# The delta rule's triangular inverse: blocks up to 32 in a compact 32-column form

## What is computed

```python
a_mat = jnp.einsum('bnhid,bnhjd->bnhij', k_beta, k) * decay * strict
sol = lax.linalg.triangular_solve(eye + a_mat, rhs, left_side=True, lower=True, unit_diagonal=True)
u, w = sol[..., :dv], sol[..., dv:]
```

## Time and profile before

| | us |
|---|---|
| median of 3 runs | 1971.06 (1970.66 to 1971.6) |
| span of the profiled execution | 1968.8 |
| one turn of the mixer loop with a chain (7 of them) | 68.6 |
| VectorE busy in such a turn | 57.3 |
| ScalarE busy in such a turn | 36.4 |
| GpSimd busy in such a turn | 1.1 |
| granted TensorE clock, mean | 0.997 |
| a load of 1024 KB of weights, from issue to landing | 5.1 |

### The profile page before, as it was taken

One profiled execution on the slowest core, in us unless ns is written; L12 is line 12 of the kernel. 1 busy time (PEld: TensorE's weight loads), 2 busy tenths in 40 slices (PEclk: granted clock), 3 DMA queues, 4 the chain that ended last, 5 costly groups with the idle time before them and its releaser, 6 DMA issues.

```text
span 1968.8 us, 30310 instructions
## 1 busy us (share of the span) xinstructions
PE 1940.8 (99%) x10837; PEld 1691.3 (86%) x10837; DVE 1289.1 (65%) x2362; ACT 984.7 (50%) x1930; POOL 28.4 (1%) x52
## 2 busy tenths in 40 slices
PE   8999999999999999999999999999999999999996
PEld 7889999999999988888888788888888888888885
DVE  6558788888878856565566697555555555555554
ACT  4446455545545535454444464544544444544442
POOL 1000000000000000000000000000000000000000
PEclk9999999999999999999999999999999999999998
DMA  8666455345445446566556555665555555665551
GB/s 314 198 159 182 124 127 147 107 118 149 111 128 133 161 142 243 193 198 199 191 191 240 172 192 188 197 201 185 187 191 191 192 192 182 223 204 195 194 195 68
DMA packets 203603, 349.51 MB, mean 178 GB/s; under 512 B 6704, under 2 KB 72448, under 8 KB 202512
## 3 DMA queue, kind: packets, MB, share of 16 engines
q1 hardware_dynamic: 200272, 334.13, 51.6%
q0 software_dynamic: 3264, 14.47, 4.5%
HBM read 344.19 MB, written 2.10 MB: 176 GB/s over the span
## 4 chain that ended last, share of the span: by engine, by line
PE 95%; DVE 2%; ACT 1%; issue 1%; DMA 0%; DVEq 0%; SPq 0%
PE dense L549 23%; PE dense L551 23%; PE dense L550 23%; PE dense L537 6%; PE dense L539 6%; PE dense L538 6%; PE chain L675 1%; PE chain L696 1%; PE chain L766 1%; PE chain L951 0%; ACT sE L1145 0%; PE chain L776 0%; PE chain L784 0%; DMA raw<-in_w_in_dram 0%; PE chain L639 0%
## 5 line engine op out<-in xcount | busy, mean ns | idle before, releaser
L1306 DVE TENSOR_TENSOR lo<-raw,hi 128x512 fp32r<-128x512 f32 x1256 | 849.9, 690 | 502.3 <-ACT hi L994 500.0
L994 ACT ACTIVATE hi<-raw 128x512 fp32r<-128x512 f32 x1256 | 780.7, 631 | 694.0 <-PE dense L551 622.9
L549 PE MATMUL dense<-hi,xh 128*128 128x512 f32 x1376 | 539.8, 392 | 1.9 <-DVE xl L1839 1.1
L551 PE MATMUL dense<-lo,xh 128*128 128x512 f32 x1376 | 535.9, 389 | 0.0
L550 PE MATMUL dense<-hi,xl 128*128 128x512 f32 x1376 | 535.5, 389 | 0.0
L549 PEld LDWEIGHTS dense<-hi,xh 128*128 128x128 f32 x1376 | 258.4, 188 | 55.2 <-DVE xl L1839 2.0
L551 PEld LDWEIGHTS dense<-lo,xh 128*128 128x128 f32 x1376 | 258.2, 188 | 54.2
L537 PE MATMUL dense<-xh,hi 128*128 128x256 f32 x1024 | 304.4, 297 | 0.0
L550 PEld LDWEIGHTS dense<-hi,xl 128*128 128x128 f32 x1376 | 258.5, 188 | 52.5
L539 PE MATMUL dense<-xh,lo 128*128 128x256 f32 x1024 | 289.6, 283 | 0.0
L538 PE MATMUL dense<-xl,hi 128*128 128x256 f32 x1024 | 289.3, 283 | 0.0
(11 more groups left out here) (290 smaller groups left out, 1521.5 us busy)
## 6 DMA issues: line engine op xcount, KB each, us to landing
raw<-in_w_in_dram SPq DMA_DIRECT2D x116, 1024.0 KB, 5.1
raw<-in_w_ffn_gate_dram SPq DMA_DIRECT2D x44, 1024.0 KB, 5.1
raw<-in_w_ffn_up_dram SPq DMA_DIRECT2D x44, 1024.0 KB, 5.1
raw<-in_w_ffn_down_dram SPq DMA_DIRECT2D x44, 1024.0 KB, 5.0
raw<-in_w_br_att_dram SPq DMA_DIRECT2D x16, 1024.0 KB, 5.0
raw<-in_w_br_dn_dram SPq DMA_DIRECT2D x16, 1024.0 KB, 5.0
raw<-in_w_out_dram SPq DMA_DIRECT2D x16, 1024.0 KB, 5.0
raw<-in_w_ple_gate_dram SPq DMA_DIRECT2D x16, 1024.0 KB, 5.0
```

What stands on the lines that cost most here:

```text
L549: pe.matmul(o, ah, hi[:, s, :], start=(k == 0), stop=False)
L551: mm = pe.matmul(o, ah, lo[:, s, :], start=False, stop=(k == nk - 1))
L994: act.activation(hi[:, pos.slot(n), :], raw[:, slot, off:off + 512], ACT.Copy).then_inc(sem("hi_ready"), 1)
L1306: dve.tensor_tensor(lo[:, pos.slot(n), :], raw[:, slot, off:off + 512], hi[:, pos.slot(n), :].bitcast(F32), ALU.subtract).then_inc(sem("lo ...
```

## The change

Levels 0 to 4 no longer work on 128 columns. In a compact form only the diagonal 32x32 blocks are kept: `VU` holds, for each of the four matrices, three blocks of 32 columns (what is left of A's own diagonal block as a level's input, the neighbour block for the level from 32 to 64, and the inverse so far). One level is then one product of 96 columns for each of the four matrices, with a stationary matrix `Ym` (a negated level part plus, in the constant mask, the identity):

- ScalarE, step 3 (`packed`): six copies of 32 partitions x 128 columns out of `AT` into `VU`.
- GpSimd (`inverse_seed`), for each pair: a copy and two elementwise instructions on 128 columns, behind `packed`. The next `G` is loaded behind them.
- VectorE, step 5 (`FIRST`): `level_matrix`, a transpose of 128 columns and a masked product of 512 columns, for level 0. The three instructions of level 0 in step 2 are gone.
- TensorE: `inv_level` in steps 6, 8, 10, 12, 14 (96 columns) and 16 (32 columns, level 5). Steps 9, 11, 13, 15 and 17 have no chain product any more, nor has step 18 its four transposes. Steps 18 and 19 keep one product each (`inv_last_y`, `inv_last_x`).
- Behind each of the five, in the same step, ScalarE copies 384 columns out of PSUM into `VU` (`vu_out`) and VectorE makes the next `level_matrix` from them; in step 14 VectorE makes four transposes of one 32-partition quadrant instead, in step 16 one more; ScalarE makes two quadrant copies in step 16 and four in step 17.
- The two tanh of step 0 write to `QKT` and `bv`; `Yz` is smaller; the mask table is 256 columns (131 KB) longer; GpSimd clears `Tm` and `Um` once.

```diff
 def stage_at(k):
-    return k if k < 4 else k - 2 if k >= 6 else None
+    return k if k < 4 else k - 2 if k >= 6 else FIRST if k == 5 else None
...
+            def inverse_seed(p):
+                pool.wait_ge(sem("packed"), p + 1)
+                pool.tensor_copy(VU[:, 2], four_of(cst[:, C_UNIT:C_UNIT + 32])).then_inc(sem("seed"), 1)
+                pool.tensor_tensor(VU[:, 0], VU[:, 0], four_of(cst[:, C_OFF:C_OFF + 32]),
+                                   ALU.mult).then_inc(sem("seed"), 1)
+                pool.wait_ge(sem("seed"), 3 * p + 2)
+                pool.tensor_tensor(VU[:, 0], VU[:, 0], four_of(cst[:, C_UNIT:C_UNIT + 32]),
+                                   ALU.subtract).then_inc(sem("seed"), 1)
...
+            def inv_level(p, n):
+                pe.wait_ge(sem("y_out"), nth("y_out", n, p))
+                if n:
+                    pe.wait_ge(sem("vu_out"), nth("vu_out", n - 1, p))
+                vu = C[:, 0, 0:384].rearrange("p (v x c) -> p v x c", v=3, x=4)
                 for x in range(4):
+                    if n < 5:
+                        mm = pe.matmul(vu[:, :, x, :], Ym[:, x, :], VU[:, :, x, :], start=True, stop=True)
+                    else:
+                        mm = pe.matmul(vu[:, 0, x, :], Yz[:, 0, x, :], VU[:, 2, x, :], start=True, stop=True)
+                mm.then_inc(sem("x_prod"), 1)
...
+                elif k in (4, 6, 8, 10, 12):
+                    n = (k - 4) // 2
+                    act.wait_ge(sem("x_prod"), nth("x_prod", n, p))
+                    act.activation(VU[:].rearrange("p v x c -> p (v x c)"), C[:, 0, 0:384],
+                                   ACT.Copy).then_inc(sem("vu_out"), 1)
...
+                elif k == 3:
+                    act.wait_ge(sem("ATc"), p + 1)
+                    for q in range(4):
+                        R = quadrant(q)
+                        r = act.activation(VU[R, 0], AT[R, :, R], ACT.Copy)
+                    for q in range(0, 4, 2):
+                        r = act.activation(VU[quadrant(q), 1], AT[quadrant(q), :, quadrant(q + 1)], ACT.Copy, scale=-1.0)
+                    r.then_inc(sem("packed"), 1)
...
+            def level_matrix(p, n, v):
+                dve.transpose(flat(Vt[:]), v).then_inc(sem("v_turned"), 1)
+                dve.wait_ge(sem("v_turned"), 5 * p + n + 1)
+                dve.tensor_tensor(Ym[:].rearrange("p x (q c) -> p x q c", q=4),
+                                  Vt[:].unsqueeze(2).to_broadcast([P, 4, 4, 32]), level_mask(n),
+                                  ALU.mult).then_inc(sem("y_out"), 1)
...
+                elif k == FIRST:
+                    dve.wait_ge(sem("seed"), 3 * p + 3)
+                    level_matrix(p, 0, flat(VU[:, 0]))
+                elif k in (4, 6, 8, 10):
+                    n = (k - 4) // 2
+                    dve.wait_ge(sem("vu_out"), nth("vu_out", n, p))
+                    level_matrix(p, n + 1, flat(VU[:, 0]))
...
+                elif k == 12:
+                    dve.wait_ge(sem("vu_out"), nth("vu_out", 4, p))
+                    for q in range(0, 4, 2):
+                        a = dve.transpose(Yz[quadrant(q + 1), 0, :, quadrant(q)], flat(VU[quadrant(q), 1]))
+                    a.then_inc(sem("y_out"), 1)
+                    for q in range(2):
+                        dve.transpose(Tm[quadrant(q), :, quadrant(q)], flat(VU[quadrant(q), 2]))
+                elif k == 14:
+                    dve.wait_ge(sem("u_other"), p + 1)
+                    dve.transpose(Tm[quadrant(1), :, quadrant(0)],
+                                  Um[quadrant(0), :, quadrant(1)]).then_inc(sem("t_rows"), 1)
```

More of the change, by code:

```diff
@@ L72 @@
 C_IDENT, C_CAUSAL = 0, 128
-C_NEGMT = 256
-C_HALF = C_NEGMT + 128
-C_COS = C_HALF + 64 * 6
+C_LEVEL = 256
+C_LAST = C_LEVEL + 128 * 5
+C_OFF = C_LAST + 64
+C_UNIT = C_OFF + 32
+C_COS = C_UNIT + 32
 C_SIN = C_COS + TT * 32
@@ L308, in build, with quadrant, four_of, level_mask @@
         one = cst[:, C_ONE:C_ONE + 1]
-        negmt0 = cst[:, C_NEGMT:C_NEGMT + P]
-        half_mask = [None] + [cst[:, C_HALF + 64 * n:C_HALF + 64 * n + 64] for n in range(6)]
+        last_mask = cst[:, C_LAST:C_LAST + 64]
+        def quadrant(q):
+            return slice(32 * q, 32 * q + 32)
+        def four_of(m):
+            return m.unsqueeze(1).to_broadcast([m.shape[0], 4, m.shape[1]])
+        def level_mask(n):
+            return four(cst[:, C_LEVEL + P * n:C_LEVEL + P * n + P]).rearrange("p x (q c) -> p x q c", q=4)
         def four(m):
@@ L490, in _ @@
             pool.wait_ge(sem("pad_zero"), due("pad_zero"))
-            pool.memset(Yz[:], 0.0).then_inc(sem("y_zero"), 1)
-            decay_in(0)
[L493 to L496, removed]
+            pool.memset(VU[:, 1], 0.0)
+            pool.memset(Yz[:], 0.0)
+            pool.wait_ge(sem("k_cols"), due("k_cols"))
+            pool.memset(Tm[:], 0.0)
+            pool.memset(Um[:], 0.0).then_inc(sem("y_zero"), 1)
+            def inverse_seed(p):
[6 more added lines that the diff above has]
+                                   ALU.subtract).then_inc(sem("seed"), 1)
+            decay_in(0)
+            for p in range(PAIRS):
+                inverse_seed(p)
+                if p + 1 < PAIRS:
+                    pool.wait_ge(sem("am"), p + 1)
+                    pool.wait_ge(sem("egb"), p + 1)
+                    decay_in(p + 1)
             def gate_bias(n):
@@ L677, in inv_y, with inv_last_y, inv_last_x @@
+            def inv_last_y(p):
+                pe.wait_ge(sem("t_rows"), p + 1)
+                for x in range(4):
+                    mm = pe.matmul(C[:, 2, x * CH:x * CH + CH], AT[:, x, :], Tm[:, x, 0:CH], start=True, stop=True)
                 mm.then_inc(sem("y_prod"), 1)
-            def inv_turn(p):
+            def inv_last_x(p):
+                pe.wait_ge(sem("y_out"), nth("y_out", 6, p))
+                pe.wait_ge(sem("u_blocks"), p + 1)
+                pe.wait_ge(sem("u_other"), p + 1)
@@ L682, in inv_turn @@
                 pe.wait_ge(sem("q_eps"), p + 1)
                 for x in range(4):
[L684 to L703, removed]
+                    mm = pe.matmul(C[:, 1, x * CH:x * CH + CH], Yz[:, 1, x, :], Um[:, x, CH:P], start=True, stop=True)
@@ L705, in scan_w @@
+                mm.then_inc(sem("xt_prod"), 1)
             def scan_w(p, c):
```

112 lines of the change are left out of this document (47 added, 65 removed).

## The result

The changed kernel takes 1983.42 us (median of 4 runs, 1983.01 to 1983.54) against 1970.86 before: 1.0063 of it, with an interval of 1.0051 to 1.0075. It is slower by 12.6 us. The prediction said 1968.8 with a range of 1957 to 1979, so it missed the sign and the range. The profiled span is 1981.1 us against 1968.8, 12.3 more.

A forecast was written before the change was run, and what follows sets the result against it. TensorE, busy for 99% of the span, was taken as the bound. Each turn loses 0.23 (4.94 new waits against 3.95 work and some 0.76 old waits); 7 x 0.23 - 3.9 = -2.3 gives 1968.8, range 1957 to 1979.

The forecast's parts named there:

- The work taken off TensorE: Chain products and four transposes removed, less one more group in step 6: 3.95 less per turn.
- level 0 to level 1: Step 6's product to step 8's: 3.77 from start to start, the round through ScalarE and VectorE covered.
- Step 6: TensorE waits 2.09 a turn for level 0's matrix, because VectorE works late through its queue.
- rival (a): Steps 3 to 5: GpSimd and VectorE hinder each other, a turn loses 0.9 more, 1975.3; chance 0.27.
- Step 11: TensorE waits 1.06 before the second scores, since VectorE copies to sE only behind its chain part in step 10.
- Steps 16 and 17: TensorE waits 1.34 before the first attention transposes and 0.45 before the second half.
- the new waits: TensorE's waits in steps 6, 11, 16 and 17 together: 4.94 a turn.
- the old ones that they replace: TensorE's waits already in a turn of the kernel before, which fall away: some 0.76.
- the doubt of 0.6 a turn: Uncertainty on either side of each turn, from copies, quadrant transposes, handovers and 96 columns: 1964 to 1973.5.
- the last pair: Pair without attention and with slower steps: nothing waits, the removed work counts in full, 3.9 less.
- Rival (d): Something in the chain far dearer, as ScalarE quadrant copies or a GpSimd instruction over 0.8: 1977 to 1990; chance 0.08.
- rival (c): All new waits covered in every turn: 31.6 less, 1939.5; chance 0.05.

The follow-up runs named there:

- g: Kernel before, old inverse kept, with f's reordering of the attention on VectorE and ScalarE: 1968.57 us, 0.9986 of before.
- h: Changed kernel, second full order: beside f, level 0's matrix inside the inverse root, second exponentials behind step 14's chain, first division ahead of it: 1934.35 us, 0.9816 of before.
- a: Changed kernel with GpSimd's seed cut to its one copy, two elementwise instructions left out, so wrong numbers: 1979.35 us, 1.0042 of before.
- c: Changed kernel with VectorE's part of the attention ahead of its chain part in steps 10 and 12: 1968.45 us, 0.9985 of before.
- i: Changed kernel with 16 useless identity transposes on TensorE where it waits in step 6: 1980.05 us, 1.0044 of before.
- d: Kernel before with one added wait: in step 6 TensorE waits for VectorE's subtraction of step 4: 1992.59 us, 1.0112 of before.
- e: Changed kernel with the moves of b and c together: 1959.23 us, 0.9938 of before.
- f: Changed kernel, first full order: level 0 before inverse root, attention parts ahead of the chain, both exponentials in step 13, GpSimd copy earlier: 1967.12 us, 0.9976 of before.
- b: Changed kernel with VectorE's inverse root and bv moved from step 3 to behind level 0's matrix in step 5: 1974.06 us, 1.0016 of before.

## Why the prediction was wrong

**The work taken off TensorE: right.** Predicted 3.95 a turn. The two kernels without a single wait in the seven turns that have a chain, g with the old inverse and h with the new, take 67.97 and 64.00: 3.97. Products of 96 columns cost what those of 64 do: level 0 to level 1 without a wait is 3.76 in h, predicted 3.77.

**Step 6: right in kind, 0.39 short.** Predicted 2.09, measured 2.48 (270.38 less 267.47 + 0.43). GpSimd in VectorE's way, rival (a), is enough for the difference: a shows 0.40 for two of its three instructions, the rows 0.50 for all. I had given it 0.9.

**Step 11: right.** From level 2 to the second scores 3.41, predicted 3.39; the wait, 1.08 from start to start where 1.06 was predicted (0.93 in the view of waits), is there in each turn, and c takes it away by the swap of the two halves of step 10's queue, which was named as its cause.

**Steps 16 and 17: right in kind, short by 0.2 and 0.15.** The first transposes come 9.93 behind level 3 (9.72), the second 12.40 (12.04). VectorE comes to its four quadrant transposes 6.50 behind level 3 instead of 6.33; their 0.31 each was right, as its timeline of step 14 shows:

```profile
291.60 0.62 DVE L1619 STREAM_TRANSPOSE Yz<-VU 32x128 f32<-32x128 f32 x2
292.25 0.62 DVE L1622 STREAM_TRANSPOSE Tm<-VU 32x128 f32<-32x128 f32 x2
...
294.28 0.69 DVE L1687 TENSOR_TENSOR sE<-sE,sm 128x512 f32<-128x512 f32 x1
```

**Small things that I had not priced.** The first group behind a wait takes 0.1 more than one in a running stream: level 0 to level 1 is 3.87 in the changed kernel and 3.76 in h, second scores to level 3 2.40 and 2.30. With three or four waits a turn that is a good part of what was short. The terms add up: step 6 0.39, level 0 to 1 0.10, up to level 3 0.05, steps 16 and 17 0.36, up to step 19 0.13 gives 1.03; the turn was predicted 0.23 longer and is 1.27 longer, 1.04 apart. The kernels without waits say the same: the new waits cost 69.85 - 64.00 = 5.85 a turn instead of 4.94, and the old ones that they replace 68.58 - 67.97 = 0.61 instead of 0.76. That is 7.3 us of the 14.6 by which the time was missed. Each term is smaller than the doubt of 0.6 a turn that the sum was given; together they exceed it, because all fell on one side.

**The steps that failed: the new waits were taken too short, and the clock was no term of the sum.** The waits cost 5.85 a turn where 4.94 was predicted, and that alone turned the sign: without the clock's share the kernel would be some 4.3 slower, at about 1975, where 2.3 faster was predicted. The clock's share then put the time outside the range. The prediction charged a wait with its length. In six places TensorE then worked for about 3.4 us at half its clock, which cost 7.95 us: the other half of the miss, and more than the gain of the last pair. i takes 6.0 of them back with the chain unchanged, d brings such falls into the kernel before by a wait alone, and e, g and h, with no wait over 0.93 in the seven turns, have none. The executions that were not profiled agree: the mean granted clock is 0.992 in all four of the changed kernel, 0.994 or 0.995 in i's, and 0.996 or 0.997 in all of e, g and h. Rival (d), something in the chain that is far dearer, has the right time (1977 to 1990) but not the reason: nothing in the chain is dearer than its row said, save the four-column instructions.

**The last pair: right in kind, its gain 0.8 too small.** 4.69 less, predicted 3.9. From its `q` transposes to step 20's first product it is 43.32 instead of 47.66, 4.34 less; the other 0.35 lies behind, and its cause is open.

**The reading that was right and wasn't followed up.** The prediction found that the gain was lost to VectorE's place in the order, not to its load. It put covered work (rival (c), 1939.5) at 0.05, rightly for this change as made; h shows that the same work in another order covers all of it.

Left open: why the clock falls in one turn and not in the next behind the same wait; why the clock rises later at the start of f and of i; whether g's 0.6 and h's gain would survive in a kernel with the seed made without GpSimd, which wasn't tried.

## What to carry to other kernels

When work is taken off the bounding engine and put as a chain through two others, the gain is decided by where the chain's links stand in those engines' queues: list for each link what is queued ahead of it, and move that first. A wait of TensorE of 1.4 us or more cost more than its length in some turns here, one of under 1 us never did, so two short waits can be better than one long one, as behind step 6 in b. And what a change is worth is measured against a version in which its waits have been ordered away, as h against g (34 us), not as made (12.6 us the other way).

## What the hardware showed that was not expected

- TensorE's granted clock fell from 1.00 to 0.50 (2.4 to 1.2 GHz) behind waits of 1.42 to 2.5 us and stayed there for some 3.4 us of full work, dense products 0.22 apart instead of 0.12; each time cost 0.9 to 1.6 us. Behind waits of up to 0.93 it never did, nor behind the two of 1.28 (f and g, in the turn without a chain). With the same wait in seven turns it fell in six (f, 1.46), in two (d, 2.5), in three (c, 2.3) or in four (changed, 2.3), and it differs from one execution of a kernel to the next: c's ten took 1964.16 to 1971.57, with mean clocks of 0.996 to 0.992. No experiment tested what decides. In c's last turn a fall lasted some 7 us, with TensorE at work and at 0.50 from 610 to 616. The Trainium skill (TensorE: Matmul & The Clock Gate, "Part 1: The HAM clock gate") has the clock follow how busy TensorE has lately been, at one of two rates; the trace agrees with the two rates, 0.50 and 1.00.
- The clock's first rise isn't at the same place in each execution: dense products of 512 columns were 0.43 apart until 17.2 us in f and until 15.7 in i, but 0.23 apart from the first one, at 11.49, in the changed kernel. That cost 2 to 3 us.
- Two-input VectorE instructions of four columns took 0.27 to 0.42 instead of 0.16 beside GpSimd instructions of 128 columns, which took 0.29 (copy) and 0.46 (two inputs), and ended 0.01 to 0.02 behind these.
- A VectorE transpose of 128 columns takes as long on 32 partitions (0.31) as on 128 (0.30), and two on different partitions don't overlap: handling single quadrants costs four times what the whole tile does.
- The first group of products behind a wait takes 0.1 longer than in a running stream (3.87 against 3.76, 2.40 against 2.30).
